# First input and weight loads in 256 KB pieces in order of use, last products in five parts, in a one-core decoder block on Trainium2

## The reference, cut to what matters

```python
h = rms_norm(x, norm1_gain[l])
proj = h @ w_in[l]                       # (256, 1024) @ (1024, 3088)
parts = [proj[..., IN_OFFSETS[i]:IN_OFFSETS[i + 1]] for i in range(len(IN_SIZES))]
...                                      # gated linear attention, MoBA attention
x = x + jnp.concatenate([o_gla, o_moba], axis=-1) @ w_out[l]
h = rms_norm(x, norm2_gain[l])
x = x + (jax.nn.silu(h @ w_ffn_gate[l]) * (h @ w_ffn_up[l])) @ w_ffn_down[l]
return rms_norm(x, final_norm_gain)
```

## Time and profile before

| | |
|---|---|
| median of 3 runs | 319.28 us (319.04 to 319.45) |
| span of the profiled execution | 317.4 us, first to last instruction |
| what lies around the span | 1.9 us, the median less the span; the page gives no other time of that execution |
| PE busy | 306.4 us (97% of the span) |
| DVE, ACT, GpSimd busy | 179.4, 153.4, 21.2 us |
| chain that ended last | PE 94% of it |

### The profile page before, as it was taken

How to read it: one execution, slowest core, us unless ns; L and a number is a source line. 1 busy time by engine, 2 the same in 40 slices (tenths; PEclk the granted TensorE clock), 3 DMA queues, 4 the chain that set the end, 5 groups by cost and what they waited for, 6 DMA issues and landing times.

```text
span 317.4 us, 3950 instructions
## 1 busy us (share of the span) xinstructions
PE 306.4 (97%) x1466; PEld 253.7 (80%) x1466; DVE 179.4 (57%) x201; ACT 153.4 (48%) x185; POOL 21.2 (7%) x44
## 2 busy tenths in 40 slices
PE   5899999999999999999999999999999999999992
PEld 5787888888877888888888888888888888888881
DVE  0788969986692527819080817364453627180434
ACT  2878797569443255535160708080715243352114
POOL 6130100000202000600000000000000000000002
PEclk9999999999999999999999999999999999999998
DMA  7986385537734300764647291909091837430003
GB/s 216 361 270 247 119 281 179 218 134 263 254 117 161 114 21 0 234 231 157 241 122 276 73 325 37 353 11 356 36 316 80 261 136 234 162 132 0 2 0 133
DMA packets 36449, 54.45 MB, mean 172 GB/s; under 512 B 2834, under 2 KB 25540, under 8 KB 36436
## 3 DMA queue, kind: packets, MB, share of 16 engines
q1 hardware_dynamic: 36356, 54.24, 50.5%
q0 software_dynamic: 64, 0.03, 0.2%
q10 hardware_dynamic: 16, 0.00, 0.0%
HBM read 53.23 MB, written 1.05 MB: 171 GB/s over the span
## 4 chain that ended last, share of the span: by engine, by line
PE 94%; DMA 2%; DVE 1%; ACT 1%; issue 0%; SPq 0%; POOLq 0%; POOL 0%; DVEq 0%
PE acc L433 15%; PE acc L435 15%; PE acc L434 15%; PE aux L435 13%; PE aux L433 13%; PE aux L434 13%; PE aux L522 4%; DMA raw<-in_w_in 2%; PE aux L627 1%; PE aux L630 1%; PE aux L600 1%; DVE x_sb L1201 1%; PE aux L582 1%; PE aux L568 1%; DVE reuse_e L1259 0%; ACT reuse_e L981 0%
## 5 line engine op out<-in xcount | busy, mean ns | idle before, releaser
L1004 DVE TENSOR_TENSOR w_lo<-raw,w_hi 128x2048 fp32r<-128x2048 f32 x48 | 107.8, 2286 | 15.6 <-ACT w_hi L789 15.6
L789 ACT CAST w_hi<-raw 128x2048 fp32r<-128x2048 f32 x48 | 89.8, 1913 | 7.1 <-PE acc L435 5.0
L433 PE MATMUL aux<-w_hi,aT_hi 128*128 128x512 f32 x176 | 69.7, 396 | 0.0
L435 PE MATMUL aux<-w_hi,aT_lo 128*128 128x512 f32 x176 | 68.7, 390 | 0.0
L434 PE MATMUL aux<-w_lo,aT_hi 128*128 128x512 f32 x176 | 68.5, 389 | 0.0
L433 PE MATMUL acc<-w_hi,aT_hi 128*128 128x512 f32 x136 | 54.7, 402 | 1.1 <-DVE w_lo L1020 1.1
L435 PE MATMUL acc<-w_hi,aT_lo 128*128 128x512 f32 x136 | 53.1, 391 | 0.0
L434 PE MATMUL acc<-w_lo,aT_hi 128*128 128x512 f32 x136 | 53.0, 390 | 0.0
L1233 DVE TENSOR_TENSOR pT_lo<-aux,pT_hi 128x512 fp32r<-128x512 f32 x10 | 6.9, 691 | 70.4 <-ACT pT_hi L950 70.4
L950 ACT CAST pT_hi<-aux 128x512 fp32r<-128x512 f32 x10 | 5.9, 587 | 76.4 <-PE aux L522 76.4
L435 PEld LDWEIGHTS aux<-w_hi,aT_lo 128*128 128x128 f32 x176 | 33.0, 188 | 7.1
(11 more groups left out here) (170 smaller groups left out, 244.2 us busy)
## 6 DMA issues: line engine op xcount, KB each, us to landing
raw<-in_w_in SPq DMA_DIRECT2D x24, 512.0 KB, 4.8
raw<-in_w_ffn_gate SPq DMA_DIRECT2D x22, 512.0 KB, 4.5
raw<-in_w_ffn_up SPq DMA_DIRECT2D x22, 512.0 KB, 5.7
raw<-in_w_ffn_down SPq DMA_DIRECT2D x22, 512.0 KB, 6.1
raw<-in_w_out SPq DMA_DIRECT2D x8, 512.0 KB, 3.9
x_sb<-in_x SPq DMA_DIRECT2D x2, 512.0 KB, 3.7
out<-reuse_e SPq DMA_DIRECT2D x4, 256.0 KB, 2.3
reuse_a<-in_final_norm_gain SPq DMA_DIRECT2D x1, 512.0 KB, 4.4
```

Source lines behind the costliest of these rows:

```text
L433: nc.tensor.matmul(dst, left_hi[:, k, tok], right_hi, start=first, stop=False)
L435: return nc.tensor.matmul(dst, left_lo[:, k, tok], right_hi, start=False, stop=last)
L789: nc.scalar.copy(w_hi[:, slot % RING, :], raw[:, slot % RAW, :]).then_inc(hi_ready, 1)
L1004: nc.vector.tensor_tensor(w_lo[:, slot % RING, :], raw[:, slot % RAW, :], w_hi[:, slot % RING, :].bitcast(f32), ALU.subtract).then_inc(lo_ ...
```

## The change

At the start, `x` comes in four pieces of 256 columns (both tiles) and the first two weight units in eight row blocks of 256 KB, issued in the order x0, w0, w1, x1, w2, w3, x2, x3, w4 to w7. PE transposes piece 0, does row block 0, transposes piece 1, does row blocks 1 and 2, transposes pieces 2 and 3, does 3 to 5, then the small products, then 6 and 7. ACT and DVE split each row block by itself. GpSimd builds `ident` ahead of its two loads. At the end, the last tile's right half is made in two parts of 256 columns, the last in another bank (`aux`); six matmuls of the unit before are moved between, and ACT issues the right halves' stores itself.

```diff
+EARLY = 2
+X_PARTS = 4
+X3_PARTS = ((0, 0, 512), (0, 512, 1024), (1, 0, 512), (1, 512, 768), (1, 768, 1024))
+SHARE = (512, 576)
...
-            for t in range(T):
-                sp.dma_start(x_sb[:, t, :], x[0, t * P:(t + 1) * P, :]).then_inc(x_loaded[t], 16)
+            def x_part(p):
+                cols = slice(p * 2 * P, (p + 1) * 2 * P)
+                sp.dma_start(x_sb[:, :, cols], x[0, :, cols].rearrange("(t p) n -> p t n", p=P)).then_inc(x_loaded[p], 16)
+
+            def first_part(n):
+                sp.dma_start(raw[:, n // 4, (n % 4) * 512:(n % 4 + 1) * 512],
+                             w_in[0, n * P:(n + 1) * P, BLOCKS[0]:BLOCKS[0] + 512]).then_inc(first_loaded[n], 16)
...
+            x_transposed(0)
+            warm_up(6)
+            first_rows(0)
+            x_transposed(1)
+            first_rows(1)
+            first_rows(2)
+            x_transposed(2)
+            x_transposed(3)
+            for k in range(3, 6):
+                first_rows(k)
+            gate_low()
+            other_gains()
+            for k in range(6, KC):
+                first_rows(k)
+            logits()
+            for u in range(EARLY, IN_UNITS):
+                in_unit(u, midway.get(u, ()))
...
+            for n in range(2):
+                down_part(before, 0, 512 * n, 512 * n + 512)
             hidden_transposed(PHASES)
+            down_part(before, 1, 0, 512)
+            down_part(before, 1, 512, 768)
...
+            for t, lo, hi in X3_PARTS[:3]:
+                down_part(final, t, lo, hi, last=True).then_inc(down_in_psum, 1)
+            down_part(before, 1, 768, D)
+            down_part(final, 1, 512, 768, last=True).then_inc(down_in_psum, 1)
+            for k in range(2):
+                last = product(aux[:, 2, 0:256], k, 1, *weights(final, D, k, 768, D), k == 0, k == 1, aT_hi, aT_lo)
...
+            def out_right(t, n_gained):
                 act.wait_ge(rstd_ready, 2 * T + t + 1)
+                act.wait_ge(gained, n_gained)
+                nc.scalar.mul(out_sb[:, t, SHARE[t]:D], out_sb[:, t, SHARE[t]:D], rstd[:, 2, t:t + 1]).then_inc(out_right_ready, 1)
+                act.wait_ge(out_right_ready, t + 1)
+                act.dma_start(out[0, t * P:(t + 1) * P, SHARE[t]:D], out_sb[:, t, SHARE[t]:D]).then_inc(out_stored, 16)
 
             for n in range(3):
                 x3_squares(n)
-            out_right(0)
+            out_right(0, 2)
             x3_squares(3)
-            out_right(1)
+            x3_squares(4)
+            out_right(1, 5)
```

More of the change, by code:

```diff
@@ L367, in then @@
                 pool.wait_ge(pool_seq, n_seq[0])
+            then(nc.gpsimd.memset(ident[:, :], 0.0))
+            nc.gpsimd.affine_select(out=ident[:, :], in_=ident[:, :], compare_op=ALU.not_equal, fill=1.0, base=0,
+                                    pattern=[[-1, P]], channel_multiplier=1).then_inc(ident_built, 1)
             with nc.allow_non_contiguous_dma(reason="256 positions, one per partition and tile"):
@@ L418, in _ @@
                 wide_rstd(1, t)
[L419 to L425, removed]
+            for n, (t, lo, hi) in enumerate(X3_PARTS):
+                pool.wait_ge(x3_sums_ready, n + 1)
+                then(nc.gpsimd.tensor_scalar(ms_f[:, n:n + 1], ss_f[:, n:n + 1], 1.0 / D,
+                                             ms_f[:, n - 1:n] if lo else EPS, ALU.mult, ALU.add))
+                if hi == D:
+                    nc.gpsimd.tensor_tensor(rstd[:, 2, t:t + 1], ms_f[:, n:n + 1], minus_half[:, 0:1],
+                                            ALU.pow).then_inc(rstd_ready, 1)
         @block.tensor
@@ L682, in hidden_transposed, with down_part, hiddenT_ready, down @@
                                for t in range(T)]).then_inc(hiddenT_in_psum, 1)
-            def down(slot, j, tiles=range(T), first=False, last=False):
+            def down_part(slot, t, lo_col, hi_col, first=False, last=False):
+                left = (aT_hi, aT_lo) if last else (pT_hi, pT_lo)
+                n = lo_col // 512
+                for k in range(2):
+                    ins = product(acc[:, 2 * t + n, lo_col - 512 * n:hi_col - 512 * n], k, t,
+                                  *weights(slot, D, k, lo_col, hi_col), first and k == 0, last and k == 1, *left)
+                return ins
+            def hiddenT_ready(j):
                 pe.wait_ge(hiddenT_hi_ready, j)
                 pe.wait_ge(hiddenT_lo_ready, j)
-                hi, lo = (aT_hi, aT_lo) if last else (pT_hi, pT_lo)
-                for t in tiles:
+            def down(slot, j, first=False):
+                hiddenT_ready(j)
+                for t in range(T):
                     for n in range(2):
[L691 to L697, removed]
+                        last = down_part(slot, t, 512 * n, 512 * n + 512, first)
+                last.then_inc(unit_used, 1)
             def gate_up_phase(j, u, slot, parity):
@@ L715, in _ @@
                       9: [probs_transposed], 10: [gla_updates], 11: [lambda: heads_transposed(0, (3, 0)), gla_outputs]}
[L716 to L722, removed]
+            after = {4: [gla_transposed], 6: [gla_scores], 7: [moba_scores], 9: [moba_outputs]}
+            x_transposed(0)
[15 more added lines that the diff above has]
+                in_unit(u, midway.get(u, ()))
                 for step in after.get(u, ()):
@@ L1028, in _ @@
                 split_first(k)
-            take_xT((4, 5, 6, 7))
-            split(1)
+            take_xT((4, 5))
+            split_first(4)
+            take_xT((6, 7))
+            for n in range(5, 4 * EARLY):
+                split_first(n)
             dve.wait_ge(low_in_psum, 1)
```

159 lines of the change are left out of this document (86 added, 73 removed).

## The result

| kernel | median us | range | executions | ratio to before, 95% interval |
|---|---|---|---|---|
| before | 319.42 | 319.04 to 319.88 | 5 | |
| changed | **322.52** | 320.81 to 323.24 | 5 | 1.0082, 1.0053 to 1.0112 |

The changed kernel is slower by 0.8%, and the medians lie 3.1 us apart. Slower was forecast, and most of the places; the size was not: 320.4 us with a range to 322.4, whose end the median passes by 0.1. The five executions make two groups, 320.81 and 320.85, and 322.52, 323.08 and 323.24. The profiled one is that of 322.52 us, with a span of 320.5, so 2.0 us lie around it.

A forecast was written before the change was run, and what follows sets the result against it. PE was taken to bound the kernel, its middle unchanged, so only its arrival at unit 2 and the tail count: start +0.8 and tail +0.3 us on 319.28 gave 320.4 us, range 319.0 to 322.4.

The forecast's parts named there:

- Where the first product goes: Start: PE's first product at 7.8 us in place of 10.30, a gain of 2.5 us.
- the 5.75 of the working: Start: time at which ACT may begin after x's first four transposes, if these take 0.22 us each.
- its compromise: Start: 5.55 us taken for ACT's beginning, between 5.2 with an early clock rise and 5.75 without.
- The transposes: Start: twelve transposes now behind the first product, at 0.11 us each, cost PE 1.3 us.
- The two new waits: Start: PE waits for weights at row blocks 2 and 4, 1.05 and 0.95 us, 2.0 in sum.
- 25.5: End of the start: the time in us at which PE was to reach unit 2, 24.71 before.
- Clock stays low: Rival, chance 0.12: PE's pauses leave TensorE at its lower clock in the start; row block 0 takes 2.76 us; 322.4 us.
- The tail: After PE's last matmul: ACT's store issue and last squares, GpSimd's steps, scaling and stores come to +0.3 us.
- Loads: Start: the small pieces of x and weights land in time and set nothing, with no margin at the last.
- Pieces too small: Rival, chance 0.02: 256 KB loads land one behind the other, w7 comes 7 us late; 327 us.

The follow-up runs named there:

- run 3: Changed kernel with eleven dummy transposes in place of six between x's first piece and the first product: 321.12 us, ratio 1.0052 to before.
- Run 4: Changed kernel with ten dummies, and x's pieces 1 to 3 transposed a row block earlier: 319.54 us, ratio 1.0011 to before.
- run 1: Changed kernel with every edit of the end taken back, so new start and old end: 321.36 us, ratio 1.0063 to before.
- run 6: Run 4 with ACT's two sums of x's squares moved ahead of its cast of unit 2: 318.80 us, ratio 0.9987 to before.
- run 7: run 6 with SP instead of ACT issuing the store of tile 0's right half: 318.45 us, ratio 0.9981 to before.
- run 9: run 7 with piece 1 of x loaded directly behind piece 0, ahead of w0 and w1: 318.48 us, ratio 0.9973 to before.
- run 2: Kernel before with the edits of the end alone, so old start and new end: 319.29 us, ratio 1.0000 to before.
- run 8: Changed kernel with none of the six dummies between x's first piece and the first product: 322.59 us, ratio 1.0109 to before.
- run 5: run 2 with SP instead of ACT issuing the store of tile 0's right half: 319.31 us, ratio 1.0004 to before.

## Why the prediction was right in direction and wrong in size

- **Where the first product goes: right, 0.3 to 0.4 short.** Forecast 7.8, measured 8.11 and 8.19. L464 ran at 2.37 to 2.45, not 2.2, and ACT began at 5.89, not 5.55: the four transposes ran at the lower clock, the 5.75 of the working and not its compromise. From there it took 2.22, forecast 2.25.
- **The transposes: right.** Forecast 1.3 us, in run 3 0.35 + 0.79 = 1.14.
- **The two new waits: right.** Forecast 1.05 and 0.95 from the start that PE could have had. In run 3 products stand 0.23 apart, so 12.74 - 11.48 - 0.23 = 1.03 and 17.34 - 16.23 - 0.23 = 0.88. The profile's own 0.86 and 0.71 count only from the end of the last matmul. Run 4 took the transposes out of their place and both waits went.
- **Left out: each stop of PE has a price of its own.** The first product after a stop or a run of transposes takes 0.30 to 0.32 us to the next, not 0.23; before there was one such stop in the start, in run 3 there are four more, 0.32 us in sum. Run 3's very first product took 0.54, 0.23 more than that of before, but that is the low clock, under which it still ran. With both the sum nearly closes: 25.5 + 0.4 - 0.1 - 0.2 + 0.32 + 0.23 = 26.15, and unit 2 came at 26.36 in run 3.
- **The step that failed: the clock was taken to be up by the first product.** "Clock stays low", with a chance of 0.12, is what the profiled execution shows, and by their times three of the five. Its working was near: row block 0 2.70 us, not 2.76, and the four transposes 0.36 more, not 0.44. Its price of 2.0 us was somewhat too large. Against run 1, with the clock up from the first product on, the low clock costs 1.23 in row block 0 (2.70 against 1.47), 0.36 at the transposes and 0.23 at the next product, and the wait at row block 2 gives 0.14 back: 1.7 in all. Against run 3 it is 1.45, since run 3's first product was slow as well. The reason given for it, PE's pause of 1.2 us, measured 1.04, is borne out by run 3, which has no pause and no execution in the upper group. It isn't enough by itself, since run 1's profile pauses for 1.66 us with the clock up. What differs is when the rise comes: in profiles where PE had dummies or transposes to do it came at about 5.3 us (run 6), 5.9 (run 1), 6.4 (run 7), 8.0 (run 9) and in the product at 8.19 (run 3), 3 to 6 us after PE's first matmul. The changed kernel's pause lies from 4.7 to 5.7 us after it, so it catches the executions in which the rise comes late. That is an inference from these profiles; no run sets the moment of the rise. The weight was wrong: the working counted for an early rise that PE starts 1.4 us sooner, and set against it only in the rival that it also pauses sooner.
- **The tail: +0.3 forecast, 0 to +0.1 measured** (run 2, and 292.8 against 292.7 us from unit 2 to the end), and the terms were wrong in both directions. ACT's last read was to come 0.33 us later after PE's end and came 0.16 earlier: the issue took 0.38 us, not 0.59, and the two squares with their reads 0.73 up to the last read, not 1.10. GpSimd's steps were to stay and took 0.26 us longer, since two now follow the last squares where one did. The `rstd` came 0.09 later, not 0.3.
- **Loads: right.** In the changed kernel's profile neither PE nor ACT waits for one of the eight row blocks. The rival "Pieces too small" has nothing for it.

For the median: 320.4 forecast; a quick execution is at 320.8 to 321.6 by run 3, which the later first product and the stops explain in the main; the low clock adds 1.4 us to that in the profiled execution. Why two executions are another 0.6 to 0.7 us above it isn't known. The Trainium skill, "TensorE: Matmul & The Clock Gate", section "What's actually happening", says that the default is the throttled state and activity releases it. The rows agree: PE begins at the lower level in every profile here (first dummies 0.22 us apart) and is at the higher one later (0.11).

## What to carry to other kernels

When an operation is moved behind the first use of its engine, follow the chain that it feeds: here twelve transposes that had cost nothing behind a load wait made two waits of 1 us, and a row block ahead they made none. Keep TensorE busy with dummies up to the first real product, and count them anew when that product moves: six left a pause behind which the first six products could run at half the clock, eleven did not. But dummies in front of a load help only if it lands before they end. A gain at the start is only had if the next thing to come late is checked too, here the load of unit 2, the squares between two casts, then piece 1 of `x`, then w1.

## What the runs showed of the hardware

- The clock's rise at the start is a matter of the single execution: during the six dummies near 6 us in run 1, only at 12 us in the changed kernel, with the same instructions up to there. Once up it stayed up through pauses of 1.31 us (run 7) and 1.66 us (run 1). It was down right behind one of 1.98 us (run 6), and fell some 1.3 us behind the end of one of 2.32 (run 8). In run 8 it rose while PE did nothing: the transposes before the pause stand 0.21 us apart, as at the lower level, the products behind it 0.23, as at the higher.
- The page's clock row reads 9 in all slices for the changed kernel, though products ran at half speed until 12.0; in runs 8 and 6, where the clock fell, the second slice reads 7. A clock that has not yet risen is seen in the distance of equal matmuls, not in the row.
- ACT was held 0.34 to 0.38 us by a store issue of its own; its load issue at the start took 0.59 to 0.62.
- The first product started 5.73 or 5.74 us after PE's first matmul in the changed kernel and in runs 1, 3 and 8, at either clock and with 0, 6 or 11 dummies: the chain through ACT and DVE sets it.
- From the start of ACT's last read to the end of GpSimd's step on 128x1 it took 0.63 us before, with one step to do. With two, one for each half of the columns, it took 0.69 in run 2, 0.89 in the changed kernel and 0.91 in run 5, for the same operations.
